# Retention's group norm on ScalarE, differential attention's norms among its items, and cross-attention queries as products of rounded parts

## The chip, the cores and the metric

One core of one Trainium2 chip. The kernel is one launch for two transformer blocks over 1024 tokens of width 1024, all inputs and outputs fp32. The metric is device time in microseconds (us), as the median over runs. The core has TensorE (PE; its weight loads are shown as PEld), VectorE (DVE), ScalarE (ACT), GpSimd (POOL) and SyncE (SP), which issues most transfers. SBUF is the on-chip memory of 128 partitions, PSUM the eight banks into which TensorE writes, 512 fp32 columns each.

## The reference

Three places of it matter here; everything else of the two blocks stays as it is.

```python
# first block: retention, o is (b, s, 4 heads, 128)
mu = jnp.mean(of, -1, keepdims=True)
var = jnp.mean(jnp.square(of - mu), -1, keepdims=True)
on = ((of - mu) * lax.rsqrt(var + EPS)).reshape(b, s, RET_WIDTH)
on = on * gn_g + gn_b
return on * jax.nn.silu(g)

# second block: differential attention, 4 heads, q and k 64 wide, v 128 wide
p = probs(qb1, k1) - lam * probs(qb2, k2)
o = jnp.einsum('bhqk,bhkv->bhqv', p, v)
da = _rmsnorm(o, da_on) * (1.0 - lam_init)
...
y = jnp.concatenate([da_out, gla_out], axis=-1) @ w_o

# second block: cross attention, 4 heads of 256, memory of 256 rows
u, mn = _rmsnorm(h, norm_g), _rmsnorm(mem, norm_m)
q = _rmsnorm((u @ w_q).reshape(b, s, 4, 256), qn)
kv = mn @ w_kv
k, v = _rmsnorm(kv[..., :d], kn), kv[..., d:]
pr = jax.nn.softmax(jnp.einsum('bshd,bmhd->bhsm', q, k) * 256 ** -0.5, axis=-1)
o = jnp.einsum('bhsm,bmhd->bshd', pr, v)
```

## The kernel before

Rows are cut into eight tiles of 128 tokens. Each engine has its own instruction stream, written out by hand; a helper function per engine and stage (`pe_...`, `act_...`, `dve_...`, `pool_...`, `sp_...`) appends that engine's part, and the order of the calls is the order on the engine. Engines meet only at counters: `x.wait_ge(*name[k])` waits for the k-th event of a counter `name`, `.then_inc(name.up(), 1)` is such an event. An engine that waits holds up all that stands behind it in its stream. Matmuls with fp32 operands are run in two passes (so eight products are sixteen rows); for the large projections the kernel uses `mm3` instead: each fp32 operand is split into a rounded part (fp32r, "high") and the rounded rest ("low"), and high·high, low·high and high·low are summed, three products of one pass. All matmuls are recorded at L180 and all transposes at L191, so groups are told apart by tiles and times.

The parts around the change, in order of time:

- **Retention, then MLA's heads.** Retention's output RO (a tile's row is 4 heads x 128) has its mean and inverse deviation per row and head in `mvr2` and `rsr`. The stage of heads runs twice, for g=0 and g=1 (four heads each): per tile TensorE forms queries and keys (`pe_heads`), ScalarE copies parts of them (L1037 to L1041, `act_heads`), VectorE rotates the queries (`dve_rotate`, L613 to L621) and TensorE turns both, which ScalarE (L1023) and VectorE (L1048) copy into QT and KT. In the stage for g=0 VectorE also does the group norm of one tile of RO, a subtract (L1069) and a multiply (L1071), each 128x512, and POOL finishes it by gain, bias and the silu gate (L969, L971, L973, `pool_finish_retention`).
- **MLA's attention** (`pe_att`, `act_att`, `dve_att`). 32 items per group; item n has a head h and a row tile i and 128(i+1) keys, items in order of i. Per item: scores, mask (L1161), reduce (L1163), scaling of the bias by a `tensor_scalar` on a 128x1 tile (L1165), Exp (L1140), turned probabilities copied by ScalarE (L1149) and VectorE, values, and VectorE's eviction into AO. `dve_att` begins with a wait for all of RO (ro_ok[8]).
- **Differential attention** (`pe_da_att`, `act_da_att`, `dve_da_att`). Again 32 items, with two score maps each: two reduces (L2266), two Exps (L2239), reciprocal, the factor lambda (L2286), the mix of both maps into PC (L2293), turned probabilities copied by ScalarE (L2247, up to 512 columns) and VectorE, values into bank 6 or 7. At step n ScalarE does the Exps of item n, the copy of item n−1 and the Square of item n−2 with its row sums (L2254), VectorE evacuates item n−2 into DO (L2278). Behind the last item come Sqrt (L2257), reciprocal and eight multiplies by the inverse deviation (L2303), then the norm of the memory rows (`act_mem` L2343, `dve_mem` L2354).
- **The projection w_o** (`project`). Sixteen turns m (half th of the tokens, column block c), each four transposes, a high part on ScalarE (L1264) and a low part on VectorE (L1285); the weights come in four pieces of 1 MB into QWR and are cut into high and low (L1257, L1277). SP issues the first piece behind the loads of x (`sp_da_back1`) that wait for the last values.
- **Cross attention.** The memory's keys and values are four groups of fp32 products (`pe_ckv`); their weights CKW use three memory slots in turn, which the query weights CQW also use, so SP waits for ck_mm[8] ahead of the query weights. Then u is turned into XT, ScalarE and VectorE sharing the sixteen copies (`pe_ux`, `act_ux`, `dve_ux`), and per row tile t run two groups of eight fp32 products for the queries (`pe_q`), norms, turns, scores, softmax and values (`pe_cross`, `act_cross`, `dve_cross`).

## Time and profile before

| what | value |
|---|---|
| median of 3 runs | 3183.2 us (3180.58 to 3184.5) |
| the profiled execution's own time | 3181.94 us |
| its span in the profile | 3179.9 us |
| TensorE busy | 2957.8 us, 93% of the span |
| VectorE busy | 1866.9 us, 59% |
| ScalarE busy | 1169.1 us, 37% |
| POOL busy | 416.4 us, 13% |
| chain of work that ended last | PE 66%, DVE 14%, DMA 11%, ACT 6%, issue 3% |

Busy time says how much an engine did, the chain says what the end of the program waited for, and only the chain can be shortened. It is followed back from the last instruction: at each step to what released it, or to the instruction before it on its engine. Times in the rows are us from the start of the span, durations us, or ns where a row is a mean over a group. "x48" behind a piece counts instructions. In a row of the timeline the bracket tells how long the engine had been idle and what released it. The granted clock of TensorE over the whole execution was 0.97 of 2.4 GHz.

### The profile page before, as it was taken

The numbers are of one execution on the slowest core, as the hardware profiler recorded it, in microseconds if no ns is written. First come the engines' busy times: TensorE is split into PE (matmuls) and PEld (weight loads), VectorE is DVE, ScalarE is ACT, GpSimd is POOL, SyncE is SP. The second block draws the span as 40 slices with busy tenths as digits, with TensorE's granted clock in tenths as the row PEclk, the third lists the DMA queues.
The fourth block names the chain that finished last, engine by engine and source line by source line (L and its number), as shares of the span: only waits on it lengthen the run. The fifth ranks groups of instructions, "written<-read, shape, count | busy, mean of one in ns | idle before, by whom it ended". The sixth has DMA issues, their size and how long they took to land.

```text
span 3179.9 us, 36445 instructions
## 1 busy us (share of the span) xinstructions
PE 2957.8 (93%) x14882; PEld 2247.2 (71%) x14882; DVE 1866.9 (59%) x2793; ACT 1169.1 (37%) x1800; POOL 416.4 (13%) x243
## 2 busy tenths in 40 slices
PE   8999698999999999989998997799998969999998
PEld 3445476887888888864556985694557958887777
DVE  5775856567444444562456436621123379999998
ACT  3111344323122111142333335412233257777676
POOL 1112400004000000021000000000000026543333
PEclk9999899999999999999999999999999989999999
DMA  8320100011111111103000010104001289999996
GB/s 320 99 80 20 43 1 1 28 67 40 53 54 40 50 43 53 53 27 133 1 1 27 28 41 1 67 14 151 8 1 62 100 315 366 392 384 383 380 378 264
DMA packets 129678, 363.35 MB, mean 114 GB/s; under 512 B 14474, under 2 KB 66984, under 8 KB 104928
## 3 DMA queue, kind: packets, MB, share of 16 engines
q1 hardware_dynamic: 112976, 330.19, 28.3%
q0 software_dynamic: 16528, 30.76, 2.6%
q8 instruction: 119, 1.95, 0.2%
q14 instruction: 55, 0.45, 0.0%
HBM read 356.69 MB, written 29.38 MB: 121 GB/s over the span
## 4 chain that ended last, share of the span: by engine, by line
PE 66%; DVE 14%; DMA 11%; ACT 6%; issue 3%; POOL 0%; SPq 0%; POOLq 0%; DVEq 0%; ACTq 0%
PE PS L180 62%; PE PS L191 3%; DMA MR<-in_w_e_up 3%; DMA MR<-in_w_e_gate 3%; DMA MR<-in_w_e_down 3%; DVE ML L2872 2%; ACT BIG L2239 1%; ACT MH L2867 1%; PE PS L590 1%; DVE BIG L846 1%; DVE ST L2266 1%; DVE BIG L2293 1%; DVE XR L1592 0%; DVE ST L1163 0%; DVE BIG L1069 0%
## 5 line engine op out<-in xcount | busy, mean ns | idle before, releaser
L180 PE MATMUL PS<-BIG 128*128 128x512 f32 (+9 forms) x2704 | 781.8, 456 | 37.6 <-ACT BIG L2239 11.4
L180 PEld LDWEIGHTS PS<-BIG 128*128 128x128 f32 (+4 forms) x2704 | 397.4, 189 | 346.4 <-issue 296.2
L2872 DVE TENSOR_TENSOR ML<-MR,MH 128x2048 fp32r<-128x2048 f32 x144 | 329.5, 2300 | 29.8 <-ACT MH L2867 29.5
L180 PE MATMUL PS<-MH,MX 128*128 128x512 f32 x1024 | 322.6, 396 | 12.0 <-DVE ML L2872 9.9
L2867 ACT CAST MH<-MR 128x2048 fp32r<-128x2048 f32 x144 | 275.4, 1914 | 91.3 <-DMA MR<-in_w_e_up 43.3
L191 PE MATMUL PS<-CT,BIG 128*128 128x128 f32 (+4 forms) x1080 | 161.6, 288 | 79.3 <-DVE BIG L2293 24.7
L180 PEld LDWEIGHTS PS<-MH,MX 128*128 128x128 f32 x1024 | 189.7, 189 | 57.8 <-DVE ML L2872 18.0
L191 PEld LDWEIGHTS PS<-CT,BIG 128*128 128x128 f32 (+4 forms) x1080 | 124.3, 144 | 143.1 <-ACT BIG L1140 35.6
L180 PE MATMUL PS<-FWH,FHH 128*128 128x512 f32 x512 | 201.1, 393 | 8.0 <-DVE FWL L1444 8.0
L180 PE MATMUL PS<-FXH,FWH 128*128 128x512 f32 x512 | 201.3, 393 | 5.0 <-DVE FWL L1444 5.0
L180 PE MATMUL PS<-FXH,FWL 128*128 128x512 f32 x512 | 200.7, 392 | 0.0
L180 PE MATMUL PS<-FXL,FWH 128*128 128x512 f32 x512 | 200.6, 392 | 0.0
L180 PE MATMUL PS<-ML,MX 128*128 128x512 f32 x512 | 200.4, 391 | 0.0
L180 PE MATMUL PS<-FWH,FHL 128*128 128x512 f32 x512 | 200.4, 391 | 0.0
L180 PE MATMUL PS<-FWL,FHH 128*128 128x512 f32 x512 | 200.4, 391 | 0.0
L1440 ACT CAST FWH<-FWR 128x2048 fp32r<-128x2048 f32 x32 | 61.0, 1908 | 266.1 <-PE PS L180 266.1
L1586 DVE TENSOR_TENSOR BC<-PS,BC 128x512 f32<-128x512 f32 x128 | 88.2, 689 | 113.5 <-PE PS L180 113.5
L2896 POOL DMA_INDIRECT out<-XR,ST x32 | 90.2, 2818 | 265.7 <-DVE XR L3001 252.5
L180 PE MATMUL PS<-DWH,DXH 128*128 128x256 f32 x384 | 113.3, 295 | 9.1 <-DVE DXL L1861 4.8
L180 PEld LDWEIGHTS PS<-FWH,FHH 128*128 128x128 f32 x512 | 97.1, 190 | 29.0 <-DVE FWL L1444 8.9
L180 PEld LDWEIGHTS PS<-FXH,FWH 128*128 128x128 f32 x512 | 97.2, 190 | 25.5 <-DVE FWL L1444 5.3
L2872 DVE TENSOR_TENSOR ML<-XR,MH 128x2048 fp32r<-128x2048 f32 x48 | 109.6, 2287 | 7.1 <-ACT MH L2867 7.0
(469 smaller groups left out, 5845.1 us busy)
## 6 DMA issues: line engine op xcount, KB each, us to landing
MR<-in_w_e_gate SPq DMA_DIRECT2D x50, 1024.0 KB, 18.9
MR<-in_w_e_up SPq DMA_DIRECT2D x48, 1024.0 KB, 21.1
MR<-in_w_e_down SPq DMA_DIRECT2D x46, 1024.0 KB, 19.3
FWR<-in_w_ff SPq DMA_DIRECT2D x32, 1024.0 KB
XR<-in_w_e_down SPq DMA_DIRECT2D x18, 1024.0 KB, 18.6
BC<-in_w_ada SPq DMA_DIRECT2D x32, 512.0 KB, 3.5
XR<-in_w_e_up SPq DMA_DIRECT2D x16, 1024.0 KB, 20.7
XR<-in_w_e_gate SPq DMA_DIRECT2D x14, 1024.0 KB, 19.4
```

The source lines that it names most:

```text
L180: ins = pe.matmul(o, l, r, start=(start and n == 0), stop=(n == len(pairs) - 1), skip_group_check=True)
L191: return pe.transpose(o, i, C("ident")[0:k, 0:k])
L590: ins = pe.matmul(PS[:, t % 4, 0:416], XT[:, k, 128 * t:128 * t + 128], LW[0][:, k, :], start=k == 0, stop=k == 7, skip_group_check=True)
L846: dve.reciprocal(o, o).then_inc(vs.up(), 1)
L1440: act.copy(chunk(FWH, i), chunk(FWR, i)).then_inc(fc_hi.up(), 1)
L1586: dve.tensor_tensor(o, PS[:, 4 + k_ % 4, :], GT2[:, 512 * n:512 * n + 512], ALU.mult).then_inc(vs.up(), 1)
L2239: act.activation(PB1[n % 2][m][:, 0:nk], sflat(n, m)[:, 0:nk], ACT.Exp, bias=bi, accum_out=rs).then_inc(da_e.up(), 1)
L2266: dve.tensor_reduce(da_sm(n, m)[1], sflat(n, m)[:, 0:nk], AX, ALU.max, negate=True).then_inc(da_b.up(), 1)
L2293: dve.scalar_tensor_tensor(out=pc, in0=PB1[n % 2][1][:, 0:nk], scalar=c2, in1=PB1[n % 2][0][:, 0:nk], op0=ALU.mult, op1=ALU.add).then_inc( ...
L2867: act.copy(cut_at(MH, i), raw(i)).then_inc(e.w_hi.up(), 1)
L2872: dve.tensor_tensor(cut_at(ML, i), raw(i), cut_at(MH, i).bitcast(F32), ALU.subtract).then_inc(e.w_lo.up(), 1)
L2896: gps.indirect_dma_start(out[0], rows_of(e, j), OB[j % NO], None, bounds_check=1023, oob_is_err=False).then_inc(e.o_out[j % NO].up(), 16)
```

## The change

Three parts that don't touch one another.

1. **Group norm.** VectorE's subtract and multiply per tile are removed. `act_norm_retention` does the same as four Identity activations per tile (scale `rsr`, bias `nbr`, one head each) behind ScalarE's copies in the stage of g=0; `nbr`, minus mean times inverse deviation, is one more small VectorE operation. POOL's finish is called behind the stage and waits for the last rotation (m_rot[8]). `dve_att` no longer waits for ro_ok[8] at its start; each eviction into AO waits for ro_ok[i+1] of its row tile. An `Exp` on the tile `ce` stands ahead of the last turn's copy, so that the Exp table is loaded there.
2. **Differential attention.** ScalarE's Square and VectorE's evacuation are done one step later (item n−3), and the Square stands ahead of the copy of the turned probabilities. Half of the norms move into the items: Sqrt of the first 16 columns at step 20, their reciprocal at step 22, the multiplies of tiles 0 to 3 at steps 23 to 26, the memory rows' norm at steps 24 (ScalarE) and 27 (VectorE). The mean and epsilon are folded into Sqrt's scale and bias. In the projection w_o the column blocks are turned in the order 4, 5, 6, 7, 0, 1, 2, 3, and only the last four wait for the differential norms.
3. **Cross attention.** Queries use `mm3`: CXH and CXL hold the high and low parts of u for 512 tokens at a time, CWH and CWL those of the query weights, which are cast and subtracted in four pieces (`act_cw`, `dve_cw`) among the memory's keys and values. CKW uses slots 2 and 3, so that the query weights are loaded early into slots 6 and 7. Turns m=0 to 7 stand ahead of the queries, turns m=8 to 15, over two banks, inside row tile t=3.

```diff
@@ first block
+            dve.scalar_tensor_tensor(out=nbr, in0=mvr2[:, :, 0], scalar=-1.0, in1=rsr, op0=ALU.mult,
+                                     op1=ALU.mult).then_inc(rs_nb.up(), 1)
...
+        def act_norm_retention(t):
+            for h in range(4):
+                o, k = RO[:, t, 128 * h:128 * h + 128], 4 * t + h
+                ins = act.activation(o, o, ACT.Identity, scale=rsr[:, k:k + 1], bias=nbr[:, k:k + 1])
+            ins.then_inc(ro_n.up(), 1)
+
+        def pool_finish_retention(heads_turned):
+            G.wait_ge(*heads_turned)
...
                     if t:
                         act_turn_heads(t - 1)
+                    if g == 0:
+                        A.wait_ge(*rs_nb[1])
+                        act_norm_retention(t)
+                if g == 0:
+                    A.wait_ge(*cs_ok[1])
+                    act.activation(ce, ce, ACT.Exp).then_inc(as_.up(), 1)
                 act_turn_heads(7)
...
-                    if g == 0:
-                        o3 = h4(RO[:, t, :])
-                        dve.tensor_tensor(o3, o3, b4(mvr2[:, 4 * t:4 * t + 4, 0], 128), ALU.subtract).then_inc(vs.up(), 1)
-                        V.wait_ge(*vs.last)
-                        dve.tensor_tensor(o3, o3, b4(rsr[:, 4 * t:4 * t + 4], 128), ALU.mult).then_inc(ro_n.up(), 1)
...
             dve_heads()
+            if g == 0:
+                pool_finish_retention(m_rot[8])
...
             def dve_att():
-                V.wait_ge(*ro_ok[8])
...
                         V.wait_ge(*o_pe[k + 1])
+                        V.wait_ge(*ro_ok[i + 1])
@@ differential attention
+                if n >= 3:
+                    k = n - 3
+                    h, i = ITEMS[k]
+                    A.wait_ge(*da_o[k + 1])
+                    A.wait_ge(*da_sq.last)
+                    A.wait_ge(*da_r[k + 1])
+                    act.activation(SQD, PS[:, 6 + k % 2, 0:128], ACT.Square, scale=da_sm(k, 0)[3],
+                                   accum_out=dos[:, i, h:h + 1]).then_inc(da_sq.up(), 1)
                 if 1 <= n <= NI:
...
-                if n >= 2:
-                    k = n - 2
...
+                if n == 20:
+                    act_da_std(0, 16)
+                if n == 24:
+                    act_mem()
+            act_da_std(16, 32)
...
+                if n == 22:
+                    dve_da_inverse(0, 16)
+                if 23 <= n < 27:
+                    dve_da_normed(n - 23)
+                if n == 27:
+                    dve_mem()
+            dve_da_inverse(16, 32)
+            for t in range(4, 8):
+                dve_da_normed(t)
@@ cross attention
-            P.wait_ge(*cq_in[n][1])
...
-            mm(PS[:, n, :], [(XT[:, k, 128 * t:128 * t + 128], CQW[n][0][:, k, :]) for k in range(8)]).then_inc(cq_mm.up(), 1)
+            wh, wl = (x[:, 4096 * n:4096 * n + 4096].rearrange("p (k n) -> p k n", k=8) for x in (CWH, CWL))
+            c0 = 128 * (t % 4)
+            P.wait_ge(*cw_lo[2 * n + 2])
+            P.wait_ge(*ux_lo[8 * (t // 4) + 8])
             P.wait_ge(*cq_ok[t])
+            mm3(PS[:, n, :], [(CXH3[:, k, c0:c0 + 128], CXL3[:, k, c0:c0 + 128], wh[:, k, :], wl[:, k, :])
+                              for k in range(8)]).then_inc(cq_mm.up(), 1)
...
-                if t < 7:
+                if t == 3:
+                    for m in range(8, 12):
+                        pe_ux(m)
+                elif t < 7:
                     pe_q(t + 1, 0)
...
+                if t == 3:
+                    for m in range(12, 16):
+                        pe_ux(m)
+                    pe_q(4, 0)
                 if t < 7:
                     pe_q(t + 1, 1)
```

How the order moves, at three places. First ScalarE, from the last tile of the stage of heads, g=0, to the first item of MLA's attention. Before:

```order
L1041 COPY BIG<-PS 128x256
L1023 COPY BIG<-PS 96x4x128 x2
L1140 ACT_TABLE_LOAD
L1140 ACTIVATE BIG,ST<-PS,ST 128x128 x2
L1149 COPY BIG<-PS 128x128
```

With the change:

```order
L1046 COPY BIG<-PS 128x4x64
L1048 COPY BIG<-PS 128x4x64
L1049 COPY BIG<-ST 128x4x32
L1050 COPY BIG<-PS 128x256
L1032 COPY BIG<-PS 96x4x128
L969 ACTIVATE BIG<-BIG,ST 128x128 x4
L1058 ACT_TABLE_LOAD
L1058 ACTIVATE ST<-ST 128x8
L1032 COPY BIG<-PS 96x4x128
L1152 ACTIVATE BIG,ST<-PS,ST 128x128 x2
```

The four norms, the table load and its small Exp now stand ahead of the last turn's copy, and no table load is left ahead of the first item's Exp. BIG is the large area of SBUF, ST the area of small columns, PS PSUM.

Second ScalarE again, step 20 of differential attention (waits in brackets; counters that are reused show under an older name: r_silu is the reduce's da_b, o_ev and ab1_ok are da_c). Before:

```order
L2239 ACTIVATE BIG,ST<-PS,ST 128x768 [waits o_ev,r_silu]
L2239 ACTIVATE BIG,ST<-PS,ST 128x768 [waits r_silu]
L2247 COPY BIG<-PS 128x512 [waits r_g]
L2254 ACTIVATE BC,ST<-PS,ST 128x128 [waits nl_ok,xt3_a,r_in]
```

With the change:

```order
L2277 ACTIVATE BIG,ST<-PS,ST 128x768 [waits r_silu]
L2285 ACTIVATE BC,ST<-PS,ST 128x128 [waits nl_ok,xt3_a,r_in]
L2293 COPY BIG<-PS 128x512 [waits r_g]
L2265 ACT_TABLE_LOAD
L2265 ACTIVATE ST<-ST 128x16
L2277 ACT_TABLE_LOAD [waits ab1_ok]
L2277 ACTIVATE BIG,ST<-PS,ST 128x768 [waits r_silu] x2
```

The Square (L2254 before, L2285 now) has changed places with the copy, and the Sqrt with a table load on either side stands behind them, ahead of the Exps of step 21.

Third TensorE, cross attention, row tile t=3. Before:

```order
L191 MATMUL PS<-CT,BC 128x128 x8
L180 MATMUL PS<-BIG,BC 128x256 x8
L191 MATMUL PS<-CT,BC 128x128 x8
L180 MATMUL PS<-BIG 128x512 x8
L180 MATMUL PS<-BIG,BC 128x256 x8
L180 MATMUL PS<-BIG 128x512 x8
```

With the change:

```order
L191 MATMUL PS<-CT,BC 128x128 x8
L180 MATMUL PS<-BIG,BC 128x256 x8
L191 MATMUL PS<-CT,BC 128x128 x8
L191 MATMUL PS<-CT,BIG 128x128 x16
L180 MATMUL PS<-BIG,BC 128x256 x8
L191 MATMUL PS<-CT,BIG 128x128 x16
L180 MATMUL PS<-CWH,CXH 128x512
L180 MATMUL PS<-CWH,CXL 128x512
L180 MATMUL PS<-CWL,CXH 128x512
```

The query products of row tile 4 (128x512) no longer stand around the scores (128x256 from BIG and BC, behind the turns); eight turns of u, in two lots of sixteen transposes, stand there, and the rounded products follow. CT is the area of constants, BC the area of broadcast and work tiles.

## Rows read from the trace of the kernel before

**Rows 1.** The page: the chain that ended last, share of the span by engine

```profile
PE 66%; DVE 14%; DMA 11%; ACT 6%; issue 3%; POOL 0%; SPq 0%; POOLq 0%; DVEq 0%; ACTq 0%
```

**Rows 2.** Chain, heads of g=0 to first Exp: start us, us, what

```profile
326.60 0.23 DVE BIG L613
...
332.64 1.70 DVE BIG L1069
...
374.68 1.28 ACT L1140
375.97 0.47 ACT BIG L1140 x2
```

**Rows 3.** Chain, the same stretch for g=1

```profile
470.27 0.23 DVE BIG L613
...
495.68 0.47 ACT BIG L1140 x2
```

**Rows 4.** Chain, differential attention, one item of 896 keys

```profile
1998.50 0.48 ACT BIG L2247
1998.97 0.37 ACT BC L2254 x2
...
1999.37 0.35 DVE BIG L2278
```

**Rows 5.** Timeline of the same item, ScalarE: start us, us, what [idle before <-releaser]

```profile
1996.40 1.01 ACT L2239 ACTIVATE BIG<-PS,ST 128x896 f32<-128x896 f32 x1 [2.99 <-DVE ST L2266]
```

**Rows 6.** Chain, from the memory's keys and values to the first query product

```profile
2193.93 0.44 PE PS L191 x4
2194.36 20.62 PE PS L180 x48
...
2214.99 7.86 DMA BIG<-in_w_cq
2222.86 0.35 issue
```

**Rows 7.** Timeline of g=1's heads, ScalarE

```profile
489.12 0.37 ACT L1037 COPY BIG<-PS 128x256 f32<-128x256 f32 x1 [0.84 <-PE PS L180]
```

**Rows 8.** Groups by line and shape, 1887 to 2051: | busy us, mean ns | idle before

```profile
L1264 ACT ACTIVATE QXH<-PS,ST 128x512 fp32r<-128x512 f32 x12 | 7.5, 688 | 1.2 <-PE PS L191 1.2
...
L1285 DVE SCALAR_TENSOR_TENSOR QXL<-PS,ST,QXH 128x512 fp32r<-128x512 f32 x8 | 5.4, 742 | 0.0
...
L2303 DVE TENSOR_TENSOR BIG<-BIG,ST 128x512 f32<-128x512 f32 x8 | 4.9, 683 | 0.0
...
L2343 ACT ACTIVATE BC<-BC 128x1024 f32<-128x1024 f32 x2 | 2.1, 1056 | 0.1
...
L1257 ACT CAST QWH<-QWR 128x2048 fp32r<-128x2048 f32 x1 | 1.9, 1891 | 0.0
...
L2354 DVE TENSOR_SCALAR BC<-BC,ST 128x1024 f32<-128x1024 f32 x2 | 1.4, 748 | 0.0
```

**Rows 9.** Chain, the last values and the first products of w_o

```profile
2028.30 5.07 PE PS L180 x32
...
2051.42 4.63 PE PS L180 x24
...
2056.92 2.87 PE PS L180 x24
```

**Rows 10.** Transfers issued from 2035.1 to 2035.3: KB, us to landing

```profile
QWR<-in_w_o SPq DMA_DIRECT2D x1, 1024.0 KB, 10.4
```

**Rows 11.** Chain, 24 rounded products of 128x512 in the experts' stage

```profile
2633.40 5.47 PE PS L180 x24
```

**Rows 12.** Timeline of g=0's heads: a POOL operation beside one of VectorE

```profile
330.70 1.26 POOL L971 TENSOR_TENSOR BIG<-BIG,BC 128x512 f32<-128x512 f32 x1
...
331.12 0.92 DVE L621 TENSOR_TENSOR BIG<-BIG 128x64 f32<-128x64 f32 x1
```

**Rows 13.** Line L1165, all of it: ns min/median/max, first and last start

```profile
L1165 DVE TENSOR_SCALAR ST<-ST x64: 153/153/155, 374.4 to 580.3; 128x1 f32<-128x1 f32 x64
```

More of the change, by code:

```diff
@@ L1228, in pe_turn @@
             def pe_turn(m):
-                th, c = divmod(m, 8)
+                th, c = m // 8, order[m % 8]
                 pe_ready(th, c)
@@ L2184, in da_sm, with act_mem, dve_mem @@
             return [sm[:, k + z:k + z + 1] for z in range(4)]
+        MEM = BC[:, 2048:4096].rearrange("p (t d) -> p t d", t=2)
+        mss = st("mss", 2)
+        SQC = bc(0)
+        mem_in, mem_sq, mem_std, mem_ok = fetched("mem_in"), by_act("mem_sq"), by_act("mem_std"), by_dve("mem_ok")
+        def act_mem():
+            A.wait_ge(*mem_in[1])
+            for t in range(2):
+                A.wait_ge(*mem_sq.last)
+                act.activation(SQC, MEM[:, t, :], ACT.Square, accum_out=mss[:, t:t + 1]).then_inc(mem_sq.up(), 1)
+            A.wait_ge(*mem_sq[2])
+            act.activation(mss, mss, ACT.Sqrt, scale=1.0 / 1024, bias=epsc[:, 1:2]).then_inc(mem_std.up(), 1)
+        def dve_mem():
+            V.wait_ge(*mem_std[1])
+            dve.reciprocal(mss, mss).then_inc(vs.up(), 1)
+            V.wait_ge(*vs.last)
+            for t in range(2):
+                dve.tensor_scalar(MEM[:, t, :], MEM[:, t, :], mss[:, t:t + 1], None, ALU.mult).then_inc(mem_ok.up(), 1)
         def sp_da_back0():
@@ L2227, in pe_da_att, with act_da_std @@
                                                  for j in range(i + 1)]).then_inc(da_o.up(), 1)
+        def act_da_std(a, b):
+            A.wait_ge(*da_sq[b])
+            act.activation(dosf[:, a:b], dosf[:, a:b], ACT.Sqrt, scale=1.0 / 128, bias=epsc[:, 1:2]).then_inc(dos_std.up(), 1)
         def act_da_att():
             A.wait_ge(*d_mm[48])
-            for n in range(NI + 2):
+            for n in range(NI + 3):
                 if n < NI:
@@ L2337, in pool_mem @@
             gps.dma_start(MEM, X["mem_2"][0].rearrange("(t p) d -> p t d", p=128)).then_inc(mem_in.up(), 16)
-        def act_mem():
-            A.wait_ge(*mem_in[1])
-            for t in range(2):
-                A.wait_ge(*mem_sq.last)
-                act.activation(SQC, MEM[:, t, :], ACT.Square, accum_out=mss[:, t:t + 1]).then_inc(mem_sq.up(), 1)
-            A.wait_ge(*mem_ms[1])
-            act.activation(mss, mss, ACT.Sqrt).then_inc(mem_std.up(), 1)
-        def dve_mem():
-            V.wait_ge(*mem_sq[2])
-            dve.tensor_scalar(mss, mss, 1.0 / 1024, EPS2, ALU.mult, ALU.add).then_inc(mem_ms.up(), 1)
-            V.wait_ge(*mem_std[1])
-            dve.reciprocal(mss, mss).then_inc(vs.up(), 1)
-            V.wait_ge(*vs.last)
-            for t in range(2):
-                dve.tensor_scalar(MEM[:, t, :], MEM[:, t, :], mss[:, t:t + 1], None, ALU.mult).then_inc(mem_ok.up(), 1)
         def wo2_first():
@@ L2382, in program @@
         pool_mem()
-        act_mem()
-        dve_mem()
         wo2_mm = by_pe("wo2_mm")
@@ L2507, in act_ux @@
[L2507 to L2520 removed]
+                if k:
+                    dve_cw(k - 1)
@@ new lines, in pe_ux, with act_ux @@
+        def pe_ux(m):
+            th, c = divmod(m, 8)
+            P.wait_ge(*uc_ok[4 * th + 4])
+            if th == 0:
+                P.wait_ge(*(ux_lo[m - 3] if m >= 4 else mt_ok[5 + m]))
+            else:
+                P.wait_ge(*(ux_lo[m - 1] if m >= 10 else cq_ok[4]))
+            for u_ in range(4):
+                ins = tr(PS[:, m % (4, 2)[th], 128 * u_:128 * u_ + 128], U[:, 4 * th + u_, 128 * c:128 * c + 128])
+            ins.then_inc(ux_tr.up(), 1)
+        def act_ux(m):
+            th, c = divmod(m, 8)
+            A.wait_ge(*ux_tr[m + 1])
+            A.wait_ge(*(cq_mm[8] if th else ck_mm[8]))
+            act.activation(CXH3[:, c, :], PS[:, m % (4, 2)[th], :], ACT.Copy, scale=ncr[:, c:c + 1]).then_inc(ux_hi.up(), 1)
@@ L2522, in program, with dve_ux @@
+        def dve_ux(m):
+            th, c = divmod(m, 8)
+            V.wait_ge(*ux_hi[m + 1])
+            V.wait_ge(*(cq_mm[8] if th else ck_mm[8]))
+            dve.scalar_tensor_tensor(out=CXL3[:, c, :], in0=PS[:, m % (4, 2)[th], :], scalar=ncr[:, c:c + 1],
+                                     in1=CXH3[:, c, :].bitcast(F32), op0=ALU.mult, op1=ALU.subtract).then_inc(ux_lo.up(), 1)
         sp_cross()
@@ L2525, in program @@
         dve_ckv()
-        pe_ux()
-        act_ux()
-        dve_ux()
+        cq_mm, cq_ok = by_pe("cq_mm"), by_dve("cq_ok")
+        act_cw(3)
+        for m in range(8):
+            pe_ux(m)
+            act_ux(m)
+            dve_ux(m)
+        dve_cw(3)
         CQ = bc(0)
@@ L2659, in dve_cross @@
                     dve_values(t - 1)
+                if t == 3:
+                    for m in range(8, 16):
+                        dve_ux(m)
                 V.wait_ge(*cs_mm[t + 1])
```

144 lines of the change are left out of this document (64 added, 80 removed).

## The prediction, made before the change was run

> **What bounds the kernel now.** I read the page first: on the chain of work that ended last, TensorE has 66%, VectorE 14%, DMA 11%, ScalarE 6% [rows 1]. So only work on that chain counts, and three stages of it are touched; I read the chain of each, then the timeline beside it for what else is late.
>
> Retention's group norm lies in the heads stage of MLA's first group (g=0). The chain there is VectorE row after row, with the norm's subtract L1069 in it (1.70 us) and POOL's products beside it: from the first rotation (326.60) to the first Exp of attention (375.97) it is 49.37 us [rows 2]. The second group runs the same stage without the norm: 470.27 to 495.68, 25.41 us, and is set by TensorE [rows 3].
>
> In differential attention an item's reduce, Exp, ScalarE copy L2247, square L2254 and VectorE's evacuation follow one another; ScalarE idles 2.99 us ahead of an item's first Exp [rows 4, 5]. Behind the last values comes a serial tail of norms and a transfer. In cross attention TensorE is always busy: three groups of eight fp32 products take 20.62 us, with one pause in which the query weights land [rows 6].
>
> **Group norm.** The two stages differ by 49.37 − 25.41 = 23.96 us, and what differs in the code is the two VectorE operations per tile, POOL's three, the wait of `dve_att` for ro_ok[8] and the table load, 1.28 us, ahead of the first Exp [rows 2, 3]. All leave this place. ScalarE gets 4 activations of 128x128 per tile. The nearest rows put one between 0.2 (as the narrow copies) and 0.47 us, so 0.8 to 1.9 per tile; in g=1 ScalarE idles 0.84 us behind TensorE ahead of a tile's first copy, and again, for less, ahead of its second [rows 7]; I take 1.3 us per tile as free. I take 0.25 each, 1.0 per tile, hidden. Only the last tile's norms and the early table load stand ahead of the last copy; beside VectorE's and TensorE's last turn I charge 0.45. Gain 23.96 − 0.45 = **23.5**; if a norm takes 0.47, ScalarE is late by 0.6 in 7 tiles, 4.2 less.
>
> POOL's 24 operations now follow the last rotation, beside attention. Alone one takes 1.26, so 3 of them and their gaps are about 4.0 per tile; the first is done about 4 behind the rotation, while turn, scores, the first Exp and the first values all lie ahead of the first AO eviction, and each further tile is wanted only four items later. I charge no stall; at worst the first eviction waits under 4 us.
>
> **Differential attention, each item.** The square and its evacuation come from the item before, so they wait for nothing, and the evacuation no longer follows the copy. The copy holds 0.48 of the chain [rows 4]; I take 0.46 for the 19 items that have the full 512 columns (8.7), and 0.37, 0.26 and 0.16 for four items each of 384, 256 and 128 columns (3.2). Step 2 has no square and evacuation any more, 0.37 + 0.35 by the same chain and their gaps, 0.8. TensorE's scores come near their limit in the wide items; −0.5. Together 12.2.
>
> **Differential attention, what is put in.** Step 20 gets a Sqrt between Exps: two table loads of 1.28 [rows 2] and the Sqrt, about 0.2, 2.8 us, into an idle stretch of 2.99 less 0.47 for the square that now lies there, somewhat less at 768 columns, 2.25: 0.6 shows. Step 24: two squares of 1.06 (about 1.16 with the accumulator's read), two loads, a Sqrt: 5.1 into 2.99 − 0.47 = 2.5; 2.6 shows [rows 5, 8]. VectorE gets a reciprocal, 0.2, four `normed` of 0.68 (one under ScalarE's stall, so 1.9 by their spacing), and `dve_mem`, 2 x 0.75 and a reciprocal, 1.6 [rows 8]. The stalls and these, 0.6 + 2.6 + 0.2 + 1.9 + 1.6, are 6.9. Net **5.3**; bounds 1 (the copy's time is only moved: another wait ends last) and 9 (insertions hidden but for step 24).
>
> Here a row and a rule can be weighed. The load ahead of the first Exp takes 1.28 and the Exp starts 0.01 behind it [rows 2], so a switch costs a load. The Trainium skill (ScalarE: Activation LUTs, Table sets) says to "do all the exps together, then all the sqrts", and gives a drain of about 1380 ns on top of every load; by that, an estimate, the four loads would cost 5.5 us more and the part's gain would be gone. The trace shows a load without it, so my sum goes by the row.
>
> **The tail.** From the end of the values (2028.30 + 5.07 = 2033.37) to the first product of w_o (2051.42) it is 18.05 us [rows 9]. Half the norms and the memory's norm are gone from it, and the transposes of GO (four turns) need none; ScalarE's and VectorE's chain would end some 13 us behind the values. But QWR's first MB lands 10.4 behind its issue at 2035.2 [rows 10], that is at 2045.6, 12.2 behind the values, and the cast (1.89 [rows 8]) and a subtract follow; the subtract, of the same 128x2048, I take at 2.4. 12.2 + 1.9 + 2.4 = 16.5. Gain **1.5**, not 5; the transfer is late next, since it waits for the last values as before. Bounds 0 and 4.
>
> **Cross attention.** Eight fp32 products take 20.62 / 3 = 6.87 us; 24 products of rounded parts 5.47 at the full clock [rows 6, 11]. 16 groups: 16 x 1.40 = **22.4** gained. Start: the weights no longer land behind ck_mm[8] (7.86 us of DMA and 0.36, so 8.2 behind it [rows 6]), but the last piece's cast (1.9) behind an evacuation, the first rounded part 0.69 and eight low parts of about 0.68 must end first [rows 8]: 0.5 + 1.9 + 0.7 + 5.4 = 8.5, a loss of 0.3. At t=3 eight further turns stand in TensorE's order over two banks: each pair costs a turn 0.44, a high part 0.69, a low part 0.74 and the gaps, 2.0 us [rows 6, 8]; four pairs 8.1. Row tile 4's first product waits for the last; the scores beside it run in the gaps, but they stood on the chain before, too, so all 8.1 shows; bounds 6 and 10. Net 22.4 − 0.3 − 8.1 = **14.0**, bounds 11 and 17. The casts of the weights lie beside fp32 work of 20.62 us and cost nothing while TensorE is the bound there.
>
> **Sum.** 23.5 + 5.3 + 1.5 + 14.0 = 44.3. The profiled execution took 3181.94, 1.3 under the median 3183.2. 3181.94 − 44.3 = 3137.6; I predict 3138. Everything from the mixture of experts on is only shifted.
>
> **Rivals.**
> (a) POOL meets VectorE in attention. For: POOL's L971 (1.26) stretches VectorE's 128x64 product L621 to 0.92 us in the first group, where 128x64 ones beside nothing take about 0.23 (as L613) [rows 2, 12]. Attention's bias scaling L1165 goes from SBUF to SBUF, 153 to 155 ns in all 64, never beside POOL so far [rows 13]. If it is held up like L621, some 15 items of the 32 us lose 0.65: 10 us, so 3148. Against: it has one column. The Trainium skill (SBUF — State Buffer, Who interferes with whom) calls the shared port an exclusive lock taken by two-port modes, which (VectorE: DVE Perf Modes, What auto-detection actually checks) a single SBUF source takes; no run here shows it for one column. Chance 0.10.
> (b) The insertions cost more, each load draining or the idle stretches being filled by something else. Four loads at twice their 1.28: 3138 + 5.1 = 3143. For: three of four stalls sit on a chain with no slack. Against: [rows 2]. Chance 0.07.
> (c) The norm doesn't leave the chain as it should: the group norm makes ScalarE the bound of the heads stage, or the evictions wait for POOL after all; a third of 23.5 is lost, 3146. Chance 0.03.
> (d) Slower. The pauses at the start of the queries and at t=3 let TensorE's clock fall to its lower level and it stays there in cross attention. The price is real: the first 24 products of w_o behind such a pause took 4.63 where the next 24 took 2.87 [rows 9]. If all 384 products of the queries ran at half clock, a group would take 10.94: 16 x 5.47 = 87.5 more, 3225. It decides when over half of them (44.3 of 87.5) do. Against: that start cost 1.76 us in all, and the full clock was back in the next 24 products. Chance 0.02.
>
> **How the numbers follow.** Forecast 0.78, (a) 0.10, (b) 0.07, (c) 0.03, (d) 0.02. Its own bounds: least gain 19.3 + 1 + 0 + 11 = 31, most 25 + 9 + 4 + 17 = 55; all four ends together are unlikely, so 3129 to 3146 holds the forecast, and 3151 takes in (a), (b) and (c). A measurement of this kernel can tell 0.2%, 6.4 us, from no change. Slower by that only in (d); within it, if (a), (b) and (c) add up with worse still, 0.03; faster 0.95.
>
> **What would show it.** In the profile after: the heads stage of g=0 from first rotation to first Exp near 25 us, ScalarE's norms between 0.2 and 0.47 each, the bias scaling still 153 ns beside POOL; an item's chain 0.46 shorter, ScalarE's stall behind step 24 near 2.6; first product of w_o 16.5 behind the values and released by QWR's parts; groups of 24 query products of 5.47 and a pause of about 8 us at t=3. The prediction is wrong if the bias scaling reads 0.5 or more, if the heads stage is above 30 us, if VectorE or ScalarE instead of TensorE holds the chain in cross attention outside t=3, or if the granted clock there is below 0.9.

## The result, and the profile after

The changed kernel takes 3141.98 us in the median of 4 runs (3141.08 to 3144.05), the kernel before 3183.85 (3180.58 to 3185.63): 41.9 us less, ratio 0.9872 with a 95% interval of 0.9858 to 0.9885. Forecast were 3138 in a range of 3129 to 3151.

For each stage I took the same two events from both traces and subtracted their starts; the line numbers have moved with the edit (L1140 is L1152 now, L1165 is L1176, L2239 is L2277).

```
stage, us                                        before   after   gain   forecast
first query copy of g=0 to first Exp              51.21   27.89   23.3   23.5
first reduce of diff. attention to last values   153.41  147.44    6.0    5.3
last values to first product of w_o               18.06   16.39    1.7    1.5
products of w_o                                   95.41   95.96   -0.6    0
end of w_o to first softmax Exp of cross         109.33  104.76    4.6  \
first softmax Exp of tile 0 to that of tile 7    159.52  151.33    8.2  / 14.0
from there to the end                            764.18  767.27   -3.1    0
```

Up to tile 7 of cross attention 43.7 us are gained (2415.67 − 2371.97; 0.6 of it ahead of the first stage of the table); behind it 3.1 are missing again in this pair of profiles. The stretch ahead of the first softmax Exp needs care: the 4.6 us are against one profile of the kernel before, and two other profiles with the same code there took 1.5 to 1.7 us less (see the part on cross attention below). Now the lines behind each.

Stage of heads, g=0. The timeline, VectorE and ScalarE (start us, us, engine, line, what [idle before <-releaser]); these answer to [rows 2] and [rows 7]:

```profile
325.96 0.23 DVE L613 TENSOR_TENSOR BIG<-PS,CSN 128x64 f32<-128x64 f32 x1 [1.24 <-ACT BIG L1050]
...
331.44 0.23 DVE L613 TENSOR_TENSOR BIG<-PS,CSN 128x64 f32<-128x64 f32 x1 [1.15 <-ACT BIG L1050]
...
332.48 0.23 DVE L621 TENSOR_TENSOR BIG<-BIG 128x64 f32<-128x64 f32 x1
332.63 0.68 DVE L1063 COPY BIG<-PS 96x512 f32<-96x512 f32 x1
...
331.77 1.67 ACT L969 ACTIVATE BIG<-BIG,ST 128x128 f32<-128x128 f32 x4
...
352.04 0.37 ACT L1152 ACTIVATE BIG<-PS,ST 128x128 f32<-128x128 f32 x1 [1.49 <-DVE ST L1176]
```

From the first rotation to the first Exp it is 352.04 − 325.96 = 26.1 us, where [rows 2] give 49.4. VectorE idles 1.15 to 1.24 us in each tile, L621 is at its 0.23 again (0.92 in [rows 12]), and the four norms of a tile take ScalarE 1.67 us together. POOL's operations lie beside attention now: its 24 operations run from 347.9 to 379.2, each 1.26 or 1.27 us long, and 15 of the scalings of the bias overlap them at 153 to 155 ns. POOL's third operation of the first tile, and all 64 scalings (ns min/median/max):

```profile
350.59 1.26 POOL L983 TENSOR_TENSOR BIG<-BIG 128x512 f32<-128x512 f32 x1
```

```profile
L1176 DVE TENSOR_SCALAR ST<-ST x64: 152/153/155, 351.8 to 556.4; 128x1 f32<-128x1 f32 x64
```

Differential attention around step 24, the timeline; it answers to [rows 4, 5]:

```profile
1949.96 1.07 ACT L2209 ACTIVATE BC<-BC 128x1024 f32<-128x1024 f32 x1
...
1952.07 2.08 DVE L2317 TENSOR_REDUCE ST<-PS 128x1 f32<-128x896 f32 x2
...
1952.33 1.28 ACT L2211 ACT_TABLE_LOAD   x1
...
1953.62 0.29 ACT L2211 ACTIVATE ST<-ST 128x2 f32<-128x2 f32 x1
1953.93 1.28 ACT L2277 ACT_TABLE_LOAD   x1
...
1955.23 1.01 ACT L2277 ACTIVATE BIG<-PS,ST 128x896 f32<-128x896 f32 x1
...
1957.37 3.36 PE L180 MATMUL PS<-BIG 64*128 64x512 f32 x8 [3.44 <-ACT BIG L2277]
...
1961.49 2.09 DVE L2317 TENSOR_REDUCE ST<-PS 128x1 f32<-128x896 f32 x2 [1.27 <-PE PS L180]
...
1964.80 1.77 PE L180 MATMUL PS<-BIG 64*128 64x512 f32 x8
...
1967.54 2.08 DVE L2317 TENSOR_REDUCE ST<-PS 128x1 f32<-128x896 f32 x2
```

The two Squares of the memory's rows end by 1952.3 (the first is shown); the load, the Sqrt and the second load follow without a gap. The reduces of items 25, 26 and 27 start at 1952.07, 1961.49 and 1967.54: a step of 9.42 us and one of 6.05. The long one has two parts. The Exps start late behind the memory's norm; and since TensorE has idled 3.44 us meanwhile, its next scores take 3.36 instead of 1.77. The view by stretches tells why (us, busy time and count by engine, then the granted clock, DMA share, GB/s):

```profile
1954.00:1957.30 3.30, 0.00 (x0) 0.00 (x0) 0.62 (x2) 3.29 (x6) 0.00 (x0) 0.85 0.00 0
1957.30:1961.00 3.70, 3.63 (x9) 1.53 (x10) 2.45 (x5) 0.84 (x4) 0.00 (x0) 0.50 0.02 4
```

TensorE did nothing in the first stretch, and in the second the granted clock is 0.50 of 2.4 GHz, its lower level.

The tail, ScalarE, TensorE and the transfer (KB, us to landing), against [rows 9, 10]:

```profile
2015.64 1.90 ACT L1269 CAST QWH<-QWR 128x2048 fp32r<-128x2048 f32 x1 [2.00 <-DMA QWR<-in_w_o]
...
2019.92 0.58 PE L180 MATMUL PS<-QWH,QXH 128*128 128x256 f32 x1 [4.51 <-DVE QWL L1289]
```

```profile
QWR<-in_w_o SPq DMA_DIRECT2D x1, 1024.0 KB, 10.3
```

As forecast, the cast waits for the landing of the weights, 2.00 us, and the first product comes 16.4 behind the values.

Cross attention from tile 2 to tile 4, the chain (start us, us, what), against [rows 6]:

```profile
2231.00 14.40 PE PS L180 x64
...
2274.89 0.65 PE PS L191 x4
2275.55 0.66 PE PS L191 x4
2276.20 3.46 PE PS L180 x16
2279.66 0.45 PE PS L191 x4
2280.13 0.70 ACT CXH L2562
2280.86 0.76 DVE CXL L2568
...
2281.66 0.67 PE PS L191 x4
2282.35 0.70 ACT CXH L2562
2283.08 1.42 DVE CXL L2568 x2
...
2284.54 12.51 PE PS L180 x48
```

The first row is an ordinary tile: 48 query products and the sixteen rows of scores in 14.40 us. The rest is t=3: turn, high part and low part follow one another, the scores stand as a block of 3.46 in the middle and keep the last four turns waiting, and the 48 query products behind the last low part take 12.51 us rather than 2 x 5.47, as the clock is low again:

```profile
2284.00:2288.00 4.00, 3.46 (x9) 2.77 (x10) 1.96 (x4) 2.94 (x9) 0.00 (x0) 0.58 0.00 0
2288.00:2292.00 4.00, 4.00 (x19) 3.30 (x18) 0.01 (x1) 0.36 (x2) 0.00 (x0) 1.00 0.00 0
```

### The profile page after: what moved, and what is told of

Read it like the earlier page. It is cut to its first block and busy times, and to the rows that moved or that the text cites. A ratio compares the mean times of both kernels' runs of the same rounds, so it can differ in the third digit from the quotient of the medians.

```text
span 3139.2 us, 36756 instructions
## 1 busy us (share of the span) xinstructions
PE 2930.0 (93%) x15010; PEld 2269.7 (72%) x15010; DVE 1854.1 (59%) x2789; ACT 1196.6 (38%) x1850; POOL 403.8 (13%) x243
## 5 line engine op out<-in xcount | busy, mean ns | idle before, releaser
L180 PE MATMUL PS<-BIG 128*128 128x512 f32 (+10 forms) x2448 | 665.9, 440 | 41.8 <-ACT BIG L2277 17.2
L180 PEld LDWEIGHTS PS<-BIG 128*128 128x128 f32 (+4 forms) x2448 | 347.3, 188 | 294.1 <-issue 236.2
L2936 ACT CAST MH<-MR 128x2048 fp32r<-128x2048 f32 x144 | 275.4, 1914 | 95.0 <-DMA MR<-in_w_e_up 43.2
```

Source lines behind the costliest of these rows:

```text
L180: ins = pe.matmul(o, l, r, start=(start and n == 0), stop=(n == len(pairs) - 1), skip_group_check=True)
L2936: act.copy(cut_at(MH, i), raw(i)).then_inc(e.w_hi.up(), 1)
```

## The experiments

### The three parts alone (e1, e2, e3)

The diff's three parts, each applied by itself to the kernel before. No line of one stands in another.

> Only the group norm's part of the change on the kernel before. Theory: it acts where it stands, 23.9 us between the first rotation of g=0 and the first Exp (49.4 to about 25.4), and all of it reaches the end: about 3160. Rival (part of the gain is given back in the experts' stage, which is held by transfers): 23.9 at the first Exp and at the end of the cross stage, but under 22 at the end of the span, 3162 or more.

Measured: 3161.25 us (3160.14 to 3162.18), ratio 0.9929 (0.9912 to 0.9945), against 3184.25 for the kernel before. First copy to first Exp 27.88 us, and from the first rotation 26.1 us, 23.3 less than before: the gain is there as the theory says. The rival is not settled by this pair of profiles: they differ by 23.9 us at the Exp of tile 7 but by 21.2 at the end of the span, which is its sign; by the medians 23.0 us reach the end.

> Only the differential attention's part. Theory: 6.0 us between the first reduce and the last values, 1.6 in the tail to the first product of w_o, so 7.6 in all: about 3176. The stall at step 24 is there again, near 4.0 us, with TensorE's next scores at half clock. Rival (the tail's gain needs the other parts, or the item's gain does): 6 or less, 3178.

Measured: 3174.13 us (3169.62 to 3177.19), ratio 0.9969 (0.9958 to 0.9980). In place: 6.0 us up to the last values (147.37), as in the whole change, but 3.4 in the tail instead of 1.7: the first product comes 14.63 us behind the values. The transfer tells why: w_o's first piece landed sooner than the 10.3 us of the changed kernel.

```profile
QWR<-in_w_o SPq DMA_DIRECT2D x1, 1024.0 KB, 8.5
```

So this term is set by a landing time that moves by 2 us between executions. A further 3.1 us are gained between the end of w_o and the first softmax Exp, more than half of it by the clock: the sixteen query products behind TensorE's first pause took 7.03 us here and 9.19 in the kernel before.

> Only the cross attention's part. Theory: 22.4 us from sixteen groups, less about 10 at t=3, and about 0.4 at the start: 13.0 in the stage and 3171 in all. Here the memory's norm stands behind differential attention as before, so the start of the stage should be the same. Rival (the weights' casts and early loads collide with w_o's evictions, shown as a loss ahead of the stage): under 11.

Measured: 3174.12 us (3172.66 to 3179.99), ratio 0.9973 (0.9961 to 0.9984). In place 4.7 us ahead of the first softmax Exp and 6.7 from tile 0 to tile 7 (152.83), 11.4 together: between the theory's 13 and the rival's 11. Nothing is lost ahead of the stage (w_o 95.40), so the rival's reason is out; tile 3 took 29.5 us here and 28.0 in the changed kernel, by the clock behind its pause: the 48 query products there took 13.98 us, and 12.51 in the changed kernel.

By medians the parts give 23.0, 10.1 and 10.1, 43.2 us together; the whole gave 41.9, and 43.6 in e11. They add, as far as medians can tell whose intervals are 7 to 11 us wide.

### What made the stage of heads long (e4, e5, e12)

e4 puts POOL back beside the stage and leaves the norm on ScalarE:

```diff
-            G.wait_ge(*heads_turned)
...
         act_lat_turn()
+        pool_finish_retention()
...
-            if g == 0:
-                pool_finish_retention(m_rot[8])
```

> The changed kernel with POOL's finish back beside the stage of heads, the norm still on ScalarE. If the chain was long because POOL's operations hold up VectorE's rotations (each of POOL's three beside two to three VectorE operations), the stage from the first rotation to the first Exp is above 30 us, about 25.4 plus 7 tiles by 1.0 to 1.7 (32 to 37). Rival (only VectorE's own subtract and multiply mattered): it stays within 1 us of 25.4.

Measured: first copy to first Exp 29.51 us where the changed kernel has 27.89 (27.7 and 26.1 from the first rotation); time 3144.2 in one run. The theory missed and so did the rival: POOL costs 1.6 us, not 7 to 12, and not under 1. It does hold up VectorE as before (L616 took 0.23 us with POOL away):

```profile
334.08 1.02 DVE L616 TENSOR_TENSOR BIG<-BIG 128x64 f32<-128x64 f32 x1
...
335.53 0.92 DVE L621 TENSOR_TENSOR BIG<-BIG 128x64 f32<-128x64 f32 x1
```

but without its own norm VectorE has room for most of that: a tile takes it 3.28 us here (from 333.69 to 336.97), with others between 3.00 and 3.84.

e5 is the other corner: the norm back on VectorE, POOL left behind the stage.

```diff
-                    if g == 0:
-                        A.wait_ge(*rs_nb[1])
-                        act_norm_retention(t)
...
+                    if g == 0:
+                        o3 = h4(RO[:, t, :])
+                        dve.tensor_tensor(o3, o3, b4(mvr2[:, 4 * t:4 * t + 4, 0], 128), ALU.subtract).then_inc(vs.up(), 1)
+                        V.wait_ge(*vs.last)
+                        dve.tensor_tensor(o3, o3, b4(rsr[:, 4 * t:4 * t + 4], 128), ALU.mult).then_inc(ro_n.up(), 1)
```

> The changed kernel with the norm's subtract and multiply back on VectorE in the stage of heads; POOL's finish stays behind the stage. If POOL's operations were the main price there, the stage from first rotation to first Exp is now near 30: 25.4 plus 0.68 + 0.70 in each of 7 to 8 tiles where TensorE has no slack, at most 35. If VectorE's own two operations were the main price, it is near 40 or more.

Measured: 30.56 us from first copy to first Exp, 2.7 over the changed kernel, and 28.8 from the first rotation. By the expectation this would make POOL the main price; e4 rules that out too, so neither is the price alone. The time, 3136.94 in one run, is lower than the changed kernel's although the stage is longer: the tail (14.68), cross attention with the clock up at t=3 (150.0) and the experts' stage (764.7) were all short in this execution.

e12 goes back to the kernel before and moves POOL alone:

```diff
-        def pool_finish_retention():
+        def pool_finish_retention(heads_turned):
+            G.wait_ge(*heads_turned)
...
-        pool_finish_retention()
...
             dve_heads()
+            if g == 0:
+                pool_finish_retention(m_rot[8])
...
             def dve_att():
-                V.wait_ge(*ro_ok[8])
...
+                        V.wait_ge(*ro_ok[i + 1])
```

> The kernel before with one thing changed: POOL's finish of retention stands behind the stage of heads, and AO's evictions wait for its tiles one by one; the norm stays on VectorE, and no Exp is put ahead. Theory after e4 and e5 (neither VectorE's two operations nor POOL's three are too many alone; together they hold each other up): the stage from ScalarE's first copy to the first Exp falls from 51.2 to about 30.6 and 1.3 for the table load, 32, so 19.3 us of the group norm's 23.3, and the time to about 3165. Rival (the low price in e5 needed the early table load or a shift of the work by ScalarE): above 36, 3169 or more.

Measured: 3165.98 us (3164.91 to 3167.12), ratio 0.9947 (0.9930 to 0.9963), 17.0 under the kernel before; first copy to first Exp 31.85 us. VectorE in one tile:

```profile
333.91 0.22 DVE L621 TENSOR_TENSOR BIG<-BIG 128x64 f32<-128x64 f32 x1
334.05 0.68 DVE L1048 COPY BIG<-PS 96x512 f32<-96x512 f32 x1
334.65 0.68 DVE L1069 TENSOR_TENSOR BIG<-BIG,ST 128x512 f32<-128x512 f32 x1
335.36 0.69 DVE L1071 TENSOR_TENSOR BIG<-BIG,ST 128x512 f32<-128x512 f32 x1
335.97 0.22 DVE L613 TENSOR_TENSOR BIG<-PS,CSN 128x64 f32<-128x64 f32 x1
```

As the theory said (32 and 3165). L1069 takes 0.68 us where it took 1.70 beside POOL [rows 2]. One tile of the kernel before, for comparison; it lasts 5.78 us (from 334.98 to 340.76, L613 to L613):

```profile
335.36 1.12 DVE L616 TENSOR_TENSOR BIG<-BIG 128x64 f32<-128x64 f32 x1
...
336.90 0.92 DVE L621 TENSOR_TENSOR BIG<-BIG 128x64 f32<-128x64 f32 x1
...
338.35 1.76 DVE L1069 TENSOR_TENSOR BIG<-BIG,ST 128x512 f32<-128x512 f32 x1
```

In e12 a tile takes 3.09 us (from 332.88 to 335.97), 0.07 over TensorE's 3.02. Beside POOL L616, L621 and L1069 are longer by 0.89, 0.70 and 1.08 us, and 3.09 + 2.67 is the 5.8 of the kernel before. So on VectorE the prices simply add; it is the stage that hides them, since a tile takes at least TensorE's 3.02 us. Without its norm VectorE has some 1.3 us less to do, 1.8 per tile, and even e4's stretched products bring that only to 3.28.

The four corners are 51.2 (both beside each other), 29.5 (POOL alone), 30.6 (VectorE's norm alone) and 27.9 (neither). Of the first, 1.3 us is the table load ahead of the first Exp, which e12 still has (31.85 beside e5's 30.56). The other 22.0 belonged to the pair, and undoing either half of it buys nearly all.

### The stall at step 24 (e6)

```diff
+                if n in (14, 17):
+                    act_mem_square((n - 14) // 3)
                 if n == 20:
                     act_da_std(0, 16)
-                if n == 24:
-                    act_mem()
+                    act_mem_std()
```

The two functions are the two halves of `act_mem`.

> The changed kernel with the memory rows' two Squares at steps 14 and 17 and their Sqrt behind the one at step 20; two table loads fewer, nothing at step 24. Theory: the stall of 3.97 us at step 25 to 26 goes (and with it TensorE's pause and the half clock behind it), the Squares hide in ScalarE's idle 2 to 2.5 us per step, and the second Sqrt costs 0.3 at step 20: 3.5 us less up to the last values. Rival (each Square of 1.06 us delays the Exps by itself, as ScalarE is nearly on the chain): under 2.

Measured: 3143.48 us in two runs. In place the step of 9.42 us is 6.04 now, the Squares and the Sqrt cost 0.2 us together, and TensorE doesn't pause there. The Exp of item 26, its idle time [3.12 <-DVE], and the stretch in which the clock fell instead, at item 28:

```profile
1960.81 1.01 ACT L2278 ACTIVATE BIG<-PS,ST 128x896 f32<-128x896 f32 x1 [3.12 <-DVE ST L2319]
```

```profile
1977.00:1981.00 4.00, 4.00 (x18) 1.99 (x15) 2.22 (x5) 0.10 (x1) 0.00 (x0) 0.60 0.00 0
```

That item took 7.73 us instead of 6.09, so the stage gained 1.9 of its 3.2. In e10, with the same edit, the clock did not fall there and the stage gained 3.2, near the 3.5 expected; the rival (under 2) fits e6's number but not its reason, as steps 14 to 19, with the two Squares in them, are as long as in the changed kernel. The theory holds for the stall; the whole time of e6 shows nothing of it, as its later stages (152.9 and 768.9) came out long.

### The weights of w_o early (e7)

```diff
+                    if i == 1 and tag == "wo2":
+                        sp_da_back1()
...
         dve_da_att()
-        sp_da_back1()
```

> The changed kernel with the first two pieces of w_o issued ahead of the four loads of x that wait for the last values. Theory: the tail ends 16.4 us behind the values only because the first piece lands there; early, VectorE's chain ends last: Square and Sqrt to about 2.1, reciprocal and four multiplies to 4.9, eight low parts to 11, subtract 2.3: 13.3, so 3 us less at the first product of w_o. Rival (the chain of turns is as long as the transfer): under 1. The loads of x come some 5 us later and are wanted only by the first evictions, at 24 products behind.

Measured: 3142.78 us in two runs. The first product comes 14.28 us behind the values (16.39 before the edit, 13.3 expected), and the products of w_o take 95.4 instead of 96.0, so the later rows of x are not missed. The chain is VectorE's now:

```profile
2015.59 1.89 ACT L1271 CAST QWH<-QWR 128x2048 fp32r<-128x2048 f32 x1
...
2017.51 2.29 DVE L1291 TENSOR_TENSOR QWL<-QWR,QWH 128x2048 fp32r<-128x2048 f32 x1 [1.04 <-ACT QWH L1271]
```

Most of the 1.0 beyond the 13.3 is this wait: ScalarE's cast stands behind its eighth high part, so VectorE waits 1.04 us for it. The edit makes the tail independent of the landing: 14.28 in e7 and e10, where the eight profiles of kernels with the changed tail and the old order of loads spread from 14.6 to 16.7. In each of those eight the first product comes 4.3 us behind the landing, so the landing sets it.

### Four banks at t=3 (e8), and the price of the turns (e9)

```diff
-                P.wait_ge(*(ux_lo[m - 1] if m >= 10 else cq_ok[4]))
+                P.wait_ge(*(ux_lo[m - 3] if m >= 12 else (cq_ok[4] if m < 10 else cqt_ok[8])))
...
-                ins = tr(PS[:, m % (4, 2)[th], 128 * u_:128 * u_ + 128], U[:, 4 * th + u_, 128 * c:128 * c + 128])
+                ins = tr(PS[:, m % 4, 128 * u_:128 * u_ + 128], U[:, 4 * th + u_, 128 * c:128 * c + 128])
...
```

> The changed kernel with the eight turns at t=3 over four banks instead of two. Theory: the insertion costs 10.0 us since two banks hold back the chain turn, high part, low part; with four VectorE's eight low parts of 0.75 set it: about 2.5 less between the Exps of t=2 and t=4. Rival (the price is the place, not the banks: the scores' Exps and the copies stand behind the turns on ScalarE): under 1.

Measured: 3138.75 us in two runs. Tile 0 to tile 7 takes 147.52 us, 3.8 less than the changed kernel's 151.33: 2.5 by the turns, as expected, and 1.3 by the clock, which stayed up. The chain there:

```profile
2275.44 3.46 PE PS L180 x16
...
2280.10 2.73 DVE CXL L2568 x4
...
2282.88 11.18 PE PS L180 x48
```

Four low parts in a row set it, and the 48 products take 11.18 us where they took 12.51. That the four banks keep the clock up is not shown: it stayed up in both profiles with them (e8, e10), but with two banks in e5 too (11.19 us).

e9 leaves the eight turns out, so that row tiles 4 to 7 use the rounded parts of tiles 0 to 3; its result is of no use, it prices the turns alone:

```diff
-            P.wait_ge(*ux_lo[8 * (t // 4) + 8])
+            P.wait_ge(*ux_lo[8])
...
-                if t == 3:
-                    for m in range(8, 12):
-                        pe_ux(m)
-                elif t < 7:
+                if t < 7:
                     pe_q(t + 1, 0)
...
```

> Leaves work out: row tiles 4 to 7 of cross attention take the rounded parts of tiles 0 to 3, so the eight turns at t=3 are gone and the queries stand where they do in the other tiles. It prices the insertion by itself. Theory: 20.8 us between the Exps of any two tiles, also t=2, 3 and 4, so 10.0 us less than the changed kernel there, of which some 1.5 is the half clock behind TensorE's pause. Rival (the pause is partly another wait of tile 3, such as the norm of the queries): 8 or less, and a longer step remains at t=3.

Measured: 3133.97 us in one run, 141.30 us from tile 0 to tile 7, 10.0 less than 151.33, of which 1.3 is the clock of the changed kernel behind its pause. The steps from one tile's Exp to the next are 20.8 us also around t=3, so the rival's longer step is not there:

```profile
2271.68 14.38 PE PS L180 x64
...
2286.53 1.30 DVE BC L2724 x2
```

### The three edits together (e10), and the change once more (e11)

> The changed kernel with the memory's Squares apart, w_o's first pieces early and four banks at t=3. Theory: the three act at different places and add, 3.4 + 2.7 + 3.8 = 9.9 at those places by the profiles of e6, e7 and e8, so about 10 less at the end of cross attention; the end of the span scatters by some us with the experts' stage: 3132, between 3129 and 3136. Rival (each only changes where TensorE's clock falls, and the next pause takes it back): over 3138.

Measured: 3130.49 us (3129.77 to 3137.65, 5 runs), ratio to the kernel before 0.9838 (0.9825 to 0.9852): some 10.3 to 11.5 under the changed kernel, and the fastest of the study; the theory said 3132, the rival over 3138. In place 3.2 (differential attention 144.20), 2.1 (tail 14.28) and 3.8 (tiles 147.54).

> The changed kernel unchanged, profiled a second time and timed beside e10. Theory: up to the end of cross attention the stages repeat within 2 us, and what differs between two executions is where TensorE's clock falls to its half level and how long the experts' stage takes, 767.3 us from the first Exp of tile 7 to the end in the first profile, 764 to 771 in the others: 3142 with 3138 to 3146. Rival (the stages repeat and the experts' stage too, so that the loss of 1.5 to 3 us behind cross attention belongs to the change): 767 again within 0.5.

Measured: 3140.78 us (3137.81 to 3144.40), ratio 0.9862 (0.9847 to 0.9877). All stages repeat within 0.3 us, but tile 3: tile 0 to tile 7 takes 152.86 (151.33 before), as the 48 products behind the pause took 14.03 us instead of 12.51. The experts' stage takes 767.31, so here the rival's number came true; what follows from it is below.

## Why the prediction was right

- **Group norm, 23.5 forecast, 23.3 measured.** The size came from comparing g=0 with g=1, and that held, whatever the parts behind it. Four norms took 1.67 us, 0.42 each and not 0.25, more than the 1.3 us that I called free. They were hidden by a hair: ScalarE's rows now follow one another without a gap, a tile in 3.01 us, and TensorE's pace was 3.02. So the stated reserve (4.2 us less at 0.47) was not needed, but nothing more would fit. The reason I gave, that all that differs leaves, was incomplete: by e4, e5 and e12 POOL alone costs 1.6 us and VectorE's norm alone 2.7, the table load 1.3, and the rest comes only when VectorE has both its norm and the stretch by POOL in one tile.
- **Item by item, 12.2 forecast.** Step 2 is 0.62 us shorter (0.8); steps 13 to 20 are 0.36 to 0.61 us shorter, mostly 0.48: the copy's 0.48 of [rows 4]. The narrower ones gave 0.16 to 0.38. Steps 28 to 30 gave 0.34: there the reduce starts 1.35 us behind the start of the mix, 1.20 before, which fits a wait for TensorE's scores but was not traced. With the last step, 2.1, all gains come to 14.0, 1.8 over the forecast.
- **Insertions, 6.9 forecast, 8.1 measured.** Step 20 cost 0.67 (0.6), `dve_mem` 1.52 (1.6), the three open multiplies 0.54 to 0.60 each (0.63). The step that failed is "2.6 shows" at step 24: it was 3.97. The mechanism was right, the term was too small by TensorE's part: the late Exps let it idle 3.44 us, and then its scores ran at the lower clock and VectorE waited 1.27 us more. That the part came to 6.0 where 5.3 was forecast is in part luck, as the 1.8 too little in the gains and the 1.2 too little in the insertions offset each other. Of the drain of about 1380 ns that the Trainium skill (ScalarE: Activation LUTs, What ACT_TABLE_LOAD costs) adds to each load, the trace has nothing: the Sqrt starts 0.01 us behind its load, the Exp 0.02 behind the other. By that figure of the Trainium skill, an estimate, the sum would have been 5.5 us lower.
- **The tail, 1.5 forecast, 1.7 measured**, by the landing as forecast; e2 and e7 show that it would have been 3.4 with a quicker transfer and 3.8 with another order.
- **Cross attention, 14.0 forecast, 12.8 measured.** The groups gave 1.40 us each: the softmax Exps of tiles 0, 1, 2 are 20.80 us apart where they were 23.60. The step that failed is "four pairs 8.1", which cost 10.0 us (e9). Of the 1.9 missing, 1.3 is the lower clock behind the pause (12.51 us for the 48 products, 11.18 in e8), which I had priced only as a rival; the other 0.6 lies in the turns. Nor do "the scores beside it run in the gaps": TensorE's order puts them as one block between the two lots of turns. At the start the gain of 4.6 is three groups' 4.2 and 0.4 more, where I had 0.3 less; but that is against 109.3 us in the one profile of the kernel before, and e1 and e12, with the same code there, took 107.8 and 107.6, so against them it is 1.2 to 1.4 less than the groups' 4.2. What sets those profiles apart is the clock behind TensorE's pause of 3.06 us, in which it waits for the norm of the first queries. TensorE's timeline has for the next sixteen products, first in the kernel before, then in e1 (7.62 in e12):

```profile
2242.01 9.19 PE L180 MATMUL PS<-BIG 128*128 128x512 f32 x16
```

```profile
2219.75 7.51 PE L180 MATMUL PS<-BIG 128*128 128x512 f32 x16
```

  In the changed kernel the 24 products behind the same pause took 7.32 us, and 5.73 in e9. So this term moves by some 1.6 us with where the clock falls, in either kernel, and the 4.6 of this pair can't be read finer than that.
- **Rival (a)**, POOL beside attention: fell. 152 to 155 ns for the scaling and 1.26 for POOL. In the stage of heads VectorE's products of two SBUF sources are stretched beside POOL (L616 1.02 and L621 0.92 instead of 0.23, e4), and those with one source in PSUM are not (L613 0.23). That agrees with the Trainium skill (SBUF — State Buffer, Who interferes with whom), by which a VectorE instruction with two SBUF inputs contends with a GpSimd one that reads SBUF. The lock by two-port modes, on which the rival rested, does not show on one column.
- **Rival (b)**: no more than the stall at step 24, for another reason. **Rival (c)**: fell, ScalarE kept pace. **Rival (d)**: the clock did fall at both pauses, and came back each time. Behind the first pause of the queries 24 products took 7.32 us (5.73 in e9, where it stayed up), behind the one at t=3 48 took 12.51 (11.18 in e8), in e11 14.03: 1.3 to 2.9 us a time, not 87.
- **Behind cross attention**, forecast 0: a cast of w_co's weights still starts 44.0 us earlier than before (2416.6 and 2460.6), and 40.6 are left at the end of the span. At one place in the experts' stage, the same products in both, the clock is at 0.62 in the changed kernel and at 1.00 in the kernel before:

```profile
2554.00:2558.00 4.00, 4.00 (x12) 3.14 (x12) 2.29 (x1) 1.25 (x2) 0.00 (x0) 0.62 0.74 283
```

```profile
2598.00:2602.00 4.00, 4.00 (x19) 3.31 (x18) 2.51 (x2) 2.58 (x2) 0.00 (x0) 1.00 0.73 275
```

which is 1.5 us. The fourteen profiles of this study, of thirteen kernels with the same experts' code, have 763.6 to 771.4 us for that last piece. The scatter is as large as what is missing, but it is not without an order: the four profiles without the cross-attention part (the kernel before, e1, e2, e12) have 763.6 to 766.9, 765.2 in the mean, and the ten with it 764.7 to 771.4, 767.6 in the mean; the changed kernel showed 767.3 in both of its profiles. Against that, the medians of the two timings (41.9 and 43.6 us less) leave little missing from the 43.7. So a loss of an us or two by the cross-attention part fits these profiles but is not shown, and its cause is open.

## What to carry to other kernels

When one engine stretches the operations of another beside a chain, add the stretch to that engine's own work in one tile and compare the sum with the pace of the engine that sets it: here that is 5.8 us against TensorE's 3.02, and 3.1 or 3.3 with either half gone. Moving POOL's part alone, a few lines, to a place where VectorE did not feel it bought 17 of the 23 us. Before inserting work into a loop, ask what TensorE does during the stall: behind the pauses of 1.6 and 3.4 us here the half clock cost another 1.3 to 2.9 us when it came, and it did not come every time. And spread an insertion over the idle stretches that the timeline shows (e6), rather than putting it into one.

## What was not expected

- In the stage of heads the prices don't add: 1.6 us for POOL, 2.7 for VectorE's norm, 22.0 for both. Each alone stays near TensorE's pace of 3.02 us a tile (3.00 to 3.84 in e4, 3.09 in e12), both together come to 5.78. On VectorE's own rows they do add.
- A `tensor_scalar` of one column from SBUF to SBUF takes 153 to 155 ns with POOL busy beside it and 152 to 155 without.
- Whether the clock falls is not settled by the code. The pause at t=3 is followed by the half clock in the changed kernel and not in e5, whose code is the same there (150.0 us from tile 0 to tile 7, 151.33 and 152.86 in the two profiles of the change). The 48 products behind that pause took 11.2, 12.5 or 14.0 us in the profiles with two banks. And at item 28 of e6 it fell behind a stretch in which TensorE was busy for 1.62 of 4 us, which it did not in e10 with the same items.
- A 1 MB load behind four of 512 KB landed 8.5 to 10.6 us behind its issue (e2 and e8; twelve profiles with this order of issue).
